# The end of an expert stage: returned rows and the last expert's product accumulated in one bank, square sums on GpSimd, loads reordered

## The reference, cut to what matters

```
h = rms(x, norm2) * (1 + sc2) + sh2
y = sum over the token's two experts e of  w_e * ((silu(h @ w1_e) * (h @ w3_e)) @ w2_e)
x = x + g2 * y
# the next layer, or the output:
h = x * rsqrt(mean(x * x) + eps) * ...
```

## Time and profile before

| what | us |
| --- | --- |
| median of 3 runs (2120.1 to 2122.18) | 2121.5 |
| the profiled execution's own time | 2129.73 |
| its span | 2128.0 |
| TensorE busy (95%) | 2024.6 |
| VectorE busy (35%) | 745.6 |
| ScalarE busy (22%) | 470.4 |
| GpSimd busy (3%) | 69.4 |

### The profile page before, as it was taken

The page is one execution under the profiler, slowest core; times in us unless marked ns, Lnnn a source line. Parts: engine busy times, 40 slices in busy tenths (PEclk is TensorE's granted clock), DMA queues, the critical chain, the costliest instruction groups (busy, mean ns, idle before and its releaser), DMA issues.

```text
span 2128.0 us, 29796 instructions
## 1 busy us (share of the span) xinstructions
PE 2024.6 (95%) x12706; PEld 1098.4 (52%) x12706; DVE 745.6 (35%) x1981; ACT 470.4 (22%) x926; POOL 69.4 (3%) x97
## 2 busy tenths in 40 slices
PE   6999999999999979999979999999999997999996
PEld 3444556556555544444445565665655554444443
DVE  1281676323311131222244767632331113122224
ACT  2211234344200121111023123424430012111111
POOL 0000100000000010000010010000000001000001
PEclk9999999999999989999989999999999998999998
DMA  9676561221122449999932223111313244799993
GB/s 389 251 273 260 192 241 45 87 91 73 72 106 99 198 154 346 393 392 392 389 139 79 80 86 122 45 67 65 119 60 119 93 177 167 286 391 392 392 401 109
DMA packets 43573, 416.59 MB, mean 196 GB/s; under 512 B 5424, under 2 KB 5552, under 8 KB 17328
## 3 DMA queue, kind: packets, MB, share of 16 engines
q1 hardware_dynamic: 30240, 369.56, 44.6%
q10 hardware_dynamic: 6720, 23.60, 3.1%
q0 software_dynamic: 6480, 21.51, 2.9%
HBM read 386.06 MB, written 28.58 MB: 195 GB/s over the span
## 4 chain that ended last, share of the span: by engine, by line
PE 85%; DMA 8%; DVE 2%; another core or an unknown queue 2%; ACT 1%; issue 1%; SPq 0%; POOL 0%; DVEq 0%; ACTq 0%; POOLq 0%
PE psum L740 16%; PE psum L1023 16%; PE psum L1124 9%; PE psum L1038 8%; PE psum L743 6%; PE psum L1145 6%; DMA pc<-we_in 5%; PE psum L1129 4%; PE psum L1066 4%; PE psum L658 2%; PE psum L854 2%; DMA ring<-wch_in 1%; DMA ring<-wmod_in 1%; PE psum L718 1%
## 5 line engine op out<-in xcount | busy, mean ns | idle before, releaser
L740 PE MATMUL psum<-hT,ring 128*128 128x384 f32 x1088 | 366.3, 490 | 2.0 <-ACT pc L1305 1.9
L1023 PE MATMUL psum<-hT,ring 128*128 128x384 f32 x1024 | 344.9, 490 | 0.0
L740 PEld LDWEIGHTS psum<-hT,ring 128*128 128x128 f32 x1088 | 201.7, 190 | 142.6 <-issue 16.3
L1023 PEld LDWEIGHTS psum<-hT,ring 128*128 128x128 f32 x1024 | 193.1, 191 | 132.1 <-issue 1.7
L1038 PE MATMUL psum<-pc,ring 128*128 128x384 f32 x512 | 175.6, 486 | 0.0
L1737 DVE SCALAR_TENSOR_TENSOR pc<-pc,par 128x128 f32<-128x128 f32 x480 | 159.5, 410 | 0.0
L2171 DVE TENSOR_TENSOR ytok<-pc,psum 128x384 f32<-128x384 f32 x32 | 17.7, 554 | 351.6 <-ACT pc L1575 351.6
L2127 DVE COPY scr<-psum 64x512 f32<-64x512 f32 (+1 forms) x180 | 91.8, 510 | 114.8 <-PE psum L1145 113.2
L1124 PE MATMUL psum<-ring,scr 128*64 128x512 f32 x512 | 119.0, 619 | 11.2 <-issue 10.4
L1038 PEld LDWEIGHTS psum<-pc,ring 128*128 128x128 f32 x512 | 95.4, 190 | 62.9 <-issue 1.5
L743 PE MATMUL psum<-ring,hT 128*128 128x512 f32 x288 | 126.1, 594 | 0.0
(11 more groups left out here) (341 smaller groups left out, 2096.9 us busy)
## 6 DMA issues: line engine op xcount, KB each, us to landing
ring<-we_in SPq DMA_DIRECT2D x48, 2048.0 KB, 18.0
pc<-we_in SPq DMA_DIRECT2D x48, 2048.0 KB, 18.8
ring<-wmod_in SPq DMA_DIRECT2D x42, 1024.0 KB, 6.1
ring<-wch_in SPq DMA_DIRECT2D x18, 2048.0 KB, 8.6
ring<-wgate_in SPq DMA_DIRECT2D x16, 2048.0 KB, 7.9
ring<-wbr_in SPq DMA_DIRECT2D x16, 1024.0 KB, 7.7
ring<-wtok_in SPq DMA_DIRECT2D x6, 2048.0 KB, 8.2
expert_out_rows<-scr ACTq DMA_DIRECT2D x30, 384.0 KB, 9.5
```

Source lines behind the costliest of these rows:

```text
L740: mm = pe.matmul(F[:, 0:T], wv[:, k, n * P:(n + 1) * P], hT[:, k, :], start=k == 0, stop=k == KD - 1)
L1023: mm = pe.matmul(bank(5 + n % 2)[:, 0:T], wv[:, k, (n % 4) * P:(n % 4 + 1) * P], hT[:, k, :], start=k == 0, stop=k == KD - 1)
```

## The change

- **SyncE's queue**: between the layers the wait for the last gather comes first; then the early weights, block 0, the parameters, block 1.
- **Scaling of `y_a`** moves from VectorE to ScalarE (`scale_back`), where scalings 0 and 1 stand ahead of the copy of the last expert's first half, and scaling 2 ahead of the copy of its second half.
- **TensorE**: `turn_mix` goes, and the two halves of `project(15)` follow each other. Each chunk n has a bank of its own (0, 1, 2, 3, 7, 4, 5, 6). The last-expert product opens it; then, for each token block, a product of the `y_a[t]` columns of this chunk (as weights) with the identity adds the returned rows into the same bank. The last-expert products of chunks 0 to 3 are issued before the first of these.
- **VectorE** adds each chunk's bank to `xT` once (two instructions); the 24 adds of `add_back` go.
- **Squares**: GpSimd adds squares 1 to 6 onto square 0, as in the middle of a layer, and TensorE has two products with ones instead of eight.

```
--- before
+++ after
@@ sync
                 if l + 1 < DEPTH:
+                    sp.wait_ge(back_in[NT - 1].sem, back_in[NT - 1].at(l, 32))
                     load_early(l + 1)
+                    fill(l + 1, BLOCKS[0])
                     load_params(l + 1)
-                if l + 1 < DEPTH:
-                    sp.wait_ge(back_in[NT - 1].sem, back_in[NT - 1].at(l, 32))
-                    fill(l + 1, BLOCKS[0])
                     fill(l + 1, BLOCKS[1])
@@ all engines
+        def back_bank(n):
+            return bank((0, 1, 2, 3, 7, 4, 5, 6)[n])
@@ tensor
                 project(NE - 1, 0)
-                turn_mix(0)
-                turn_mix(1)
                 project(NE - 1, 1)
-                turn_mix(2)
+                def last_back(n):
+                    pe.wait_ge(xy_ready.sem, xy_ready.at(l, 2 * NE - 1 + n // 4))
+                    pe.matmul(back_bank(n)[:, 0:T], x_last[:, n * P:(n + 1) * P], last_pickT[0:CAP, :], start=True, stop=False,
+                              skip_group_check=True)
+                for n in range(4):
+                    last_back(n)
                 for n in range(KD):
-                    pe.wait_ge(xy_ready.sem, xy_ready.at(l, 2 * NE - 1 + n // 4))
-                    if n == 0:
-                        pe.wait_ge(moe_done.sem, moe_done.at(l, 1))
-                    if n >= 2:
-                        pe.wait_ge(out_used.sem, out_used.at(l, KD + n - 1))
-                    pe.matmul(bank(n % 2)[:, 0:T], x_last[:, n * P:(n + 1) * P], last_pickT[0:CAP, :], start=True, stop=True)\
-                      .then_inc(out_done.sem, 1)
-                    if n == 2:
-                        pe.wait_ge(moe_done.sem, moe_done.at(l, 2))
-                    if n >= 2:
-                        add_square(l + 1, n - 2)
-                add_square(l + 1, KD - 2)
-                add_square(l + 1, KD - 1)
+                    if n >= 4:
+                        last_back(n)
+                    for t in range(NT):
+                        if n == 0:
+                            pe.wait_ge(mix_ready.sem, mix_ready.at(l, t + 1))
+                        mm = pe.matmul(back_bank(n)[:, tok(t)], y_a[t][:, n * P:(n + 1) * P], ident, start=False, stop=True,
+                                       skip_group_check=True)
+                    mm.then_inc(out_done.sem, 1)
+                pe.wait_ge(square_sum.sem, square_sum.at(l, 2 * (KD - 2)))
+                pe.matmul(bank(2)[:, 0:T], ones, hT[:, 0, :], start=True, stop=False)
+                pe.wait_ge(squares_ready.sem, square_count(l + 1, 0, KD))
+                pe.matmul(bank(2)[:, 0:T], ones, hT[:, KD - 1, :], start=False, stop=True).then_inc(sumsq_done.sem, 1)
@@ scalar
-                for n in range(2):
+                def scale_back(t):
+                    ac.wait_ge(back_in[t].sem, back_in[t].at(l, 32))
+                    ac.activation(y_a[t], y_a[t], ACT.Identity, scale=rt[:, 91 + t:92 + t]).then_inc(scaled_back.sem, 1)
+                def keep_last(n):
                     ac.wait_ge(xy_done.sem, xy_done.at(l, 2 * NE - 1 + n))
                     ac.activation(x_last[:, n * W:(n + 1) * W], bank(5 + n)[0:CAP, :], ACT.Copy).then_inc(xy_ready.sem, 1)
+                scale_back(0)
+                scale_back(1)
+                keep_last(0)
+                scale_back(2)
+                keep_last(1)
@@ vector
-                def mix(t):
-                    ve.wait_ge(back_in[t].sem, back_in[t].at(l, 32))
-                    step(ve.tensor_scalar(y_a[t], y_a[t], rt[:, 91 + t:92 + t], None, ALU.mult))
-                    chain.settle()
+                for t in range(NT):
+                    ve.wait_ge(scaled_back.sem, scaled_back.at(l, t + 1))
                     ve.scalar_tensor_tensor(y_a[t], y_b[t], rt[:, 94 + t:95 + t], y_a[t], ALU.mult, ALU.add)\
                       .then_inc(mix_ready.sem, 1)
...
                 for n in range(KD):
                     ve.wait_ge(out_done.sem, out_done.at(l, KD + n + 1))
                     for c, s in enumerate((CTX, LAT)):
-                        o = ve.scalar_tensor_tensor(xT[:, n, s], bank(n % 2)[:, s], mod[:, 40 + n, c:c + 1],
+                        o = ve.scalar_tensor_tensor(xT[:, n, s], back_bank(n)[:, s], mod[:, 40 + n, c:c + 1],
                                                     xT[:, n, s], ALU.mult, ALU.add)
@@ gpsimd, behind the gathers
+                for n in range(1, KD - 1):
+                    gp.wait_ge(squares_ready.sem, square_count(l + 1, 0, n + 1))
+                    if n >= 2:
+                        gp.wait_ge(square_sum.sem, square_sum.at(l, KD - 2 + n - 1))
+                    gp.tensor_tensor(hT[:, 0, :], hT[:, 0, :], hT[:, n, :], ALU.add).then_inc(square_sum.sem, 1)
```

More of the change, by code:

```diff
@@ L346, in hybrid_step @@
         squares_ready = sig("squares_ready", 0)
-        square_sum = sig("square_sum_step", KD - 2)
+        square_sum = sig("square_sum_step", 2 * (KD - 2))
         sumsq_done = sig("sumsq_done", 0)
@@ L453, in hybrid_step @@
         mix_ready = sig("token_sum_ready", NT)
-        mix_turned = sig("token_sum_turned", NT)
-        moe_done = sig("moe_added", NT)
+        scaled_back = sig("back_rows_scaled", NT)
         spill_known = sig("spill_known", 1)
@@ L476, in hybrid_step @@
         block = ctx.enter_context(nc.Block())
-        def mix_out(t, k):
-            b = 2 * t + k // 4 if t < 2 else (4, 7)[k // 4]
-            return bank(b)[:, k % 4 * P:(k % 4 + 1) * P]
+        def back_bank(n):
+            return bank((0, 1, 2, 3, 7, 4, 5, 6)[n])
         def bflip(d, t):
@@ L630, in _ @@
             pe.wait_ge(loaded.sem, 32)
[L632 to L637, removed]
             def have(l, key):
@@ L1156, in turn_hidden @@
                     pe.transpose(turned[:, :, BIG:CAP], x_g[:, 2, :], ident).then_inc(xgt_done.sem, 1)
[L1158 to L1162, removed]
                 pe.wait_ge(ht_copied.sem, ht_copied.at(l, 6))
```

## The result

| | us |
| --- | --- |
| before, median of 4 runs (2120.1 to 2122.18) | 2121.71 |
| after, median of 4 runs (2101.14 to 2101.9) | 2101.47 |
| ratio | 0.9906 (0.9889 to 0.9923) |
| the profiled execution after, its span | 2101.14, 2099.1 |

The account below looks back on a forecast made before the run. TensorE was taken to bound the kernel, with 85% of the chain of waits. Layer 1's 3.8 plus layer 0's 6.5, less 1.7 for clock, gave 8.6 us gained: 2112.9 us, range 2103.5 to 2117.5.

Parts of the forecast that it names:

- The failed step: End of the expert stage: TensorE's completions wait for POOL's last indirect transfer, so layer 0 would get layer 1's stall too.
- layer 0's gain: End of layer 0's expert stage, up to the normalisation's logarithm: 6.5 us earlier, with layer 1's stall assumed there.
- case B: No stall in layer 0, or in neither layer when unprofiled: 15.4 us gained, 2106.1 us; chance 0.30.
- The new tail: End of each layer's expert stage: halves back to back, chunk rounds, GpSimd's sum; layer 1's logarithm at about 2114.9.
- Layer 1's 3.8: End of layer 1's expert stage: logarithm at 2114.9 instead of 2118.74, a gain of 3.8 us.
- the stalled case: Layer 1's end as first profiled: ScalarE released only at 2089.23, the next product at half speed, 6.62 us.
- The clock: Start of layer 1 after the new pauses: TensorE's low clock costs between nothing and 1.7 us; 1.7 taken.
- Loads: Between the layers: small loads behind the gathers bring layer 0's gathers 5.96 us earlier; weights arrive in time, costing nothing.
- Scaling: Returned rows scaled on ScalarE at about 1.04 us each, with nothing added to the path.
- case C: GpSimd's square adds have gaps of 0.3 us: sum of squares 1.5 later a layer, 2115.9 us; chance 0.10.
- E: At the layers' ends GpSimd's and VectorE's adds block each other: 9.2 us slower, 2130.7 us; chance 0.05.

## Why the prediction was wrong

**The failed step** is "I take it as one thing: TensorE's completions can be held until POOL has issued its last indirect transfer". It made a rule of three late releases in a single execution, 8.2 us above its median, and took 6.8 us out of layer 0's gain (6.5 instead of 13.3). The runs showed that no release is late there (ScalarE released at 1064.70 and 2066.77, both halves at full speed, 7.08): it is case B, which had 0.30. The 8.2 us were the row to believe. The Trainium skill (SBUF — State Buffer, Who interferes with whom) holds that TensorE never waits on a transfer or another engine's port; in all executions but that one ScalarE was released by TensorE's own product beside the gathers, so there the trace agrees with the rule that the prediction did not follow. What made the three releases late is not known.

**Case B's own number** (15.4) was short as well, by terms:

| term | B said | measured |
| --- | --- | --- |
| layer 0's tail | 13.3 | 12.4 (35.45 - 23.08) |
| layer 1's tail | 3.8 | 5.4 (28.51 - 23.07) |
| clock at layer 1's start (measured: layer 0's exponential to that of layer 1's middle norm) | -1.7 | +1.4 (674.1 - 672.7) |
| sum | 15.4 | 19.2 |

- *The new tail* was well worked out: 22.7 from release to logarithm against 23.08. Halves 7.08 together, four chunks at 0.67 (2.84), rounds of 1.32: as said. The 0.4 are GpSimd's chain, 6.71 instead of 6.3.
- *Layer 1's 3.8* is the step that B mis-sized: it kept the old and the new tail of the stalled case. The old tail without the stall (28.5) less 22.7 would have given 5.8.
- *The clock* had the wrong sign. The prediction took the mid-layer norm of the earlier trace rows as the nearer row, with a longer low stretch. But this window of layer 1's start after the change is at 1.00, where the stretch from 1104.3 in the earlier trace rows was at half:

```profile
1090.00:1108.00 18.00, 17.28 (x53) 1.00 0.00 2
```

The clock stayed up there in all three executions of the kernel after, in the one with the loads undone and in the one with four squares on GpSimd; it fell there in all four executions with the old tail (three of the kernel before, one with the loads alone). It is no rule, though: the run with the scaling on VectorE had the pauses of the kernel after (1.56 and 2.93 us) and lost 3.1 us there, the cost that the prediction feared. What decides between the two is not shown. And the clock was no term at the edge alone: the old tails hold low stretches too (mean 0.86 and 0.94), of which the prediction counted only the slower halves of the last expert's output.
- *Remaining*: 19.2 of 20.2. From layer 0's first exponential to that of its middle norm the executions took 733.0 to 739.4 us, whatever the kernel; a difference of 1 is not to be attributed. The table compares one execution with one. With all three of the kernel after (mean tails 23.6 and 23.6) and the two unstalled ones of the kernel before (35.3 and 28.55), the tails give 16.6 and the sum is 18.0, between the two gains that were measured, 20.2 and 16.7.

**The other steps.** Loads: as said, first gather 1060.15 (said 1060.0); layer 1's weights were in time, TensorE starts its first unit at 1090.68 on ScalarE's word. Scaling: 1.15 each instead of 1.04, at no cost. GpSimd: case C was partly true. Its adds stand 1.145 apart, 0.14 between them (C said 0.3, the forecast 0.05), so the sum of squares ends last, 0.2 behind the last square, with TensorE waiting 1.58; giving two squares back to TensorE won 0.5, the four products following without a pause. The Trainium skill (SBUF — State Buffer, Who interferes with whom) says that a VectorE instruction with one SBUF input outside its two-port modes leaves GpSimd alone; 998 against 995 ns agrees, and E did not come.

**Where the 20.2 come from**, by parts, as the tails of profiled executions show it: the loads' order 3.8 (in place; 6.8 alone), the square sums 4.1, the scaling nothing. The bank is the rest of the tails, 9.9 in place (17.8 - 3.8 - 4.1), which agrees with the 10.1 that it took out of them alone. But alone its instruction list also ran into the late load of instructions, 3.7, which the kernel after, by where its list happens to end, does not; and in the median time of ten runs the bank alone is not told from the kernel before. So its share is shown in the tails, not in the time.

## What to carry to other kernels

Before a stall seen once is made a rule, compare the profiled execution's time with the median, and profile the same kernel again: the three late releases (2.4, 2.4 and 3.2 us) lay in 8 us of difference that stood on record. Price each pause of TensorE as a range, from the pause alone to the pause with slower products behind it: the same pauses left the clock up in one execution and not in another. Work out the old and the new stretch in the same case. Parts don't add up (6.8 alone, 3.8 in place), and a kernel with a few instructions more or less can gain or lose some 4 us where a burst of tiny products meets a load of instructions: a repeat with some harmless instructions added tells that from the edit's own effect, if their own cost is taken from its trace (54 small products cost 3.3 us here, not the 1.5 expected).

## What the runs showed of the hardware that was not expected

- TensorE can run dry of instructions: in a burst of 64x32 products (15 ns a record) it stood 1.95 to 2.01 us in three executions, ending 2.2 to 2.3 us after the 16 KB load began; 7 more products moved the pause by 14 records, 54 more removed it.
- Dependent adds on GpSimd (128x384, 0.998 us) stand 0.14 us apart, less than its gathers (0.30).
- Stretches at the lower clock fall on different places in executions of one kernel: the same tail took 23.1 or 24.8 us (mean clock 1.00 or 0.93), and behind the same two pauses layer 1 began at 2.4 GHz in one execution and at 1.2 GHz in another.
- TensorE's completions were reported late three times, by 2.4 to 3.2 us, in one of 15 profiled executions, with no cause in the trace.
